# Taking a transition's second root from three sums gathered in the GEMM before it, and merging the residual update into the norm, in a two-block transformer kernel

## What is computed

```
x = x + g_m[:, None, :] * rmsnorm_2(y, norm_g[l, 1])      # y: output of the mixer (short conv, or attention)
h = modulate(rmsnorm_2(x, norm_g[l, 2]), sh_f, sc_f)      # h * (1 + scale) + shift
y = squared_relu_mlp(h, mlp_up_w[l], mlp_down_w[l])
x = x + g_f[:, None, :] * rmsnorm_2(y, norm_g[l, 3])
```

## Time and profile before

| | us |
|---|---|
| median of 3 runs | 1821.46 |
| lowest, highest | 1819.21, 1821.91 |
| the profiled execution | 1821.19 |
| its span | 1818.5 |
| TensorE busy with matmuls | 1780.4 (98%) |
| VectorE busy | 1080.0 (59%) |
| ScalarE busy | 614.1 (34%) |
| GpSimd busy | 80.0 (4%) |

### The profile page before, as it was taken

The page is one execution under the profiler, slowest core; times in us unless marked ns, Lnnn a source line. Parts: engine busy times, 40 slices in busy tenths (PEclk is TensorE's granted clock), DMA queues, the critical chain, the costliest instruction groups (busy, mean ns, idle before and its releaser), DMA issues. The chain is left out here.

```text
span 1818.5 us, 22910 instructions
## 1 busy us (share of the span) xinstructions
PE 1780.4 (98%) x8160; PEld 1426.7 (78%) x8160; DVE 1080.0 (59%) x1556; ACT 614.1 (34%) x951; POOL 80.0 (4%) x132
## 2 busy tenths in 40 slices
PE   9999999999999999999999999999989999999996
PEld 7777677888888878887888888877757788888885
DVE  5566464655655566776656565658766755434354
ACT  4226444322222343223423232425344341323230
POOL 0000000000000000001000000010000100000001
PEclk9999999999999999999999999999999999999998
DMA  6231111444454434552254555422421234333321
GB/s 223 75 108 34 44 41 60 155 161 151 138 169 154 139 93 129 182 186 93 93 188 161 194 165 187 145 70 70 126 72 62 90 107 159 97 93 100 93 81 46
DMA packets 59984, 215.33 MB, mean 118 GB/s; under 512 B 6656, under 2 KB 6656, under 8 KB 59776
## 3 DMA queue, kind: packets, MB, share of 16 engines
q1 hardware_dynamic: 43632, 154.95, 25.5%
q0 software_dynamic: 16128, 58.73, 10.4%
q10 hardware_dynamic: 144, 0.59, 0.1%
HBM read 212.15 MB, written 2.10 MB: 118 GB/s over the span
## 5 line engine op out<-in xcount | busy, mean ns | idle before, releaser
L726 ACT ACTIVATE w_hi<-w_raw 128x1024 fp32r<-128x1024 f32 x285 | 300.6, 1056 | 459.6 <-PE psum L1646 416.8
L1644 PE MATMUL psum<-h_hi,w_hi 128*128 128x512 f32 x1080 | 421.6, 390 | 1.4 <-DVE h_lo L1079 0.9
L1645 PE MATMUL psum<-h_lo,w_hi 128*128 128x512 f32 x1080 | 420.2, 389 | 0.0
L1646 PE MATMUL psum<-h_hi,w_lo 128*128 128x512 f32 x1080 | 420.2, 389 | 0.0
L1048 DVE TENSOR_TENSOR w_lo<-w_raw,w_hi 128x1024 fp32r<-128x1024 f32 x285 | 348.3, 1222 | 110.9 <-ACT w_hi L726 100.7
L1646 PE MATMUL psum<-hid_hi,w_lo 128*128 128x512 f32 x760 | 295.7, 389 | 0.0
L1644 PE MATMUL psum<-hid_hi,w_hi 128*128 128x512 f32 x760 | 295.6, 389 | 0.0
L1645 PE MATMUL psum<-hid_lo,w_hi 128*128 128x512 f32 x760 | 295.6, 389 | 0.0
L1644 PEld LDWEIGHTS psum<-h_hi,w_hi 128*128 128x128 f32 x1080 | 202.7, 188 | 45.2 <-DVE h_lo L1079 1.3
L1645 PEld LDWEIGHTS psum<-h_lo,w_hi 128*128 128x128 f32 x1080 | 202.8, 188 | 42.2 <-issue 0.5
L1646 PEld LDWEIGHTS psum<-h_hi,w_lo 128*128 128x128 f32 x1080 | 202.7, 188 | 41.9
(11 more groups left out here) (279 smaller groups left out, 1933.6 us busy)
## 6 DMA issues: line engine op xcount, KB each, us to landing
w_raw<-in_wstream SPq DMA_DIRECT2D x285, 512.0 KB, 3.6
ada_raw<-in_ada POOLq DMA_DIRECT2D x112, 512.0 KB, 3.8
x<-in_xT SPq DMA_DIRECT2D x8, 256.0 KB, 6.5
outT<-x SPq DMA_DIRECT2D x8, 256.0 KB, 2.1
con<-in_consts SPq DMA_DIRECT2D x1, 1028.0 KB, 10.5
con<-in_rope ACTq DMA_DIRECT2D x1, 576.0 KB, 3.8
par<-in_params SPq DMA_DIRECT2D x1, 259.0 KB, 2.7
```

What stands on the lines that cost most here:

```text
L726: act.activation(w_hi[:, slot, :], w_raw[:, slot, :], ACT.Copy).then_inc(whi_done, 1)
L1644: pe.matmul(bank, w_hi[:, slot, w], hi[:, ra + k, :], start=k == 0, stop=False)
L1645: pe.matmul(bank, w_hi[:, slot, w], lo[:, ra + k, :], start=False, stop=False)
L1646: mm = pe.matmul(bank, w_lo[:, slot, w], hi[:, ra + k, :], start=False, stop=k == nk - 1)
```

## The change

It touches the first and the third transition; the second stays as it was.

The sum of squares of the new x = x + r * b, where b = y * gain and r is the root of y, is written out as sum(x^2) + 2 r sum(x * b) + r^2 sum(b^2). The three sums do not need r, and are gathered in the stage that makes y (`fore`). For each of its eight blocks c: ScalarE squares x[c], y[c] and y[c] * gain; VectorE copies y[c], makes b_mul = y * gain * x and adds y's square of the block before to ss; GpSimd adds the three new products to x_sum, b_sum and g_sum (19 adds in a stage, the last b and g adds are VectorE's). For blocks 6 and 7 ScalarE also multiplies y by the gain in place. The split of w_lo comes after this work instead of before it, and GpSimd issues its ada loads between the adds.

Behind the stage: TensorE takes the means of the three sums (`means`), ScalarE makes the root of y and a copy of it in SBUF, VectorE combines the means (`resum`), ScalarE takes the second root from that. The update is merged into the norm (`renew`): GpSimd finishes tiles 6 and 7 while the root is made, then tiles 1, 3 and 5; VectorE tiles 0, 2 and 4, between its norm operations. The stages squares and sums of squares of the new x go away. In the first transition four modulation groups instead of five come before take, and the group that is left out moves into the MLP (modulation(3) in place of modulation(2) behind its second group); the numbers of warming matmuls are 2 and 8 behind take.

The diff, cut to this (semaphores, counters and the choice of operands in rstd are left out):

```diff
+    def renew(groups, gain, name, shift, more, warm):
+
+
+
+        about = dict(inst=counts["fore"] // DT - 1, old=gain)
+        modulation(1)
+        total(1)
+        add("means", **about)
+        modulation(groups - 1)
+        rstd(EPS2, wide=True, fore=about["inst"] + 1)
+        add("resum", **about)
+        take()
+        gains(name)
+        modulation(more, warm, bank=3)
+        rstd(EPS2, resummed=about["inst"] + 1)
+        r0 = counts["rhs"]
+        add("renew", dict(val=DT, hi=DT, rhs=DT, step=3, xup=3, xpool=5, held=3), dst="h", src="x", src_at=0, nch=DT,
+            dst_at=0, gain=name, shift=shift, splits={}, **about)
+        return r0
...
-    close(5, "r_m0", ("g_f0",), 2, (3, 7))
-    h = norm("h", gain="g_f0", shift=24)
+    gemm("acc", 8, "hid", hid, dst="y", first=True, sq=True, fore="r_m0", rows=8)
+    h = renew(4, "r_m0", "g_f0", 24, 2, 2)
...
-    mlp(h, (0, 12, 12, 8), (16, 16, 16, 0), 2, 1)
+    mlp(h, (0, 12, 12, 8), (16, 16, 16, 0), 3, 1)
...
-    close(3, "r_m1", ("g_f1",), 0, (11, 15))
-    h = norm("h", gain="g_f1", shift=88)
+    h = renew(3, "r_m1", "g_f1", 88, 0, 8)
...
+        y_sq, g_sq, x_sq, b_mul = ([scratch[:, 2 * i + j, :] for j in range(2)] for i in range(4))
+        b_sum, g_sum, x_sum = scratch[:, 8, :], scratch[:, 9, :], rstd[:, :]
+        mean_b, mean_g, mean_x, new_root = (psum[:, i, :] for i in (0, 1, 2, PT_BANK))
+        root_copy, resum = scratch[:, 4, :], scratch[:, 0, :]
+        OWN, ADDED, WHOLE = (0, 2, 4), (1, 3, 5), (6, 7)
...
+                if s.get("fore") and s["kind"] == "gemm":
+                    inst = s["at"]["fore"] // DT
+                    for c in range(DT):
+                        if c >= 1:
+                            pool.wait_ge(fore_x, DT * inst + c + 1)
+                            pool.wait_ge(sum_x, 7 * inst + c - 1)
+                            pool.tensor_tensor(x_sum, x_sq[0] if c == 1 else x_sum, x_sq[c % 2], ALU.add).then_inc(sum_x, 1)
+                        if 1 <= c < DT - 1:
+                            pool.wait_ge(fore_b, DT * inst + c + 1)
+                            pool.wait_ge(sum_b, 6 * inst + c - 1)
+                            pool.tensor_tensor(b_sum, b_mul[0] if c == 1 else b_sum, b_mul[c % 2], ALU.add).then_inc(sum_b, 1)
+                            pool.wait_ge(fore_g, DT * inst + c + 1)
+                            pool.wait_ge(sum_g, 6 * inst + c - 1)
+                            pool.tensor_tensor(g_sum, g_sq[0] if c == 1 else g_sum, g_sq[c % 2], ALU.add).then_inc(sum_g, 1)
+                        upto = min((s["at"]["ada"] + (c + 1) * s["rows"] // DT) // 2 + 2, 4 * ADA_GROUPS)
+                        for v in range(done, upto):
+                            pool.wait_ge(ada_used, 2 * v - 2)
+                            load(v, v % 2)
+                        done = max(done, upto)
+                if s["kind"] == "resum":
+                    pool.wait_ge(root_done, s["inst"] + 1)
+                    for i, c in enumerate(WHOLE):
+                        n = len(WHOLE) * s["inst"] + i + 1
+                        pool.wait_ge(gained_done, n)
+                        pool.tensor_tensor(y[:, c, :], y[:, c, :], root_copy, ALU.mult).then_inc(gained_mul, 1)
+                        pool.wait_ge(gained_mul, n)
+                        pool.tensor_tensor(x[:, c, :], x[:, c, :], y[:, c, :], ALU.add).then_inc(x_pool, 1)
...
+                if s["kind"] == "renew":
+                    for i, c in enumerate(ADDED):
+                        pool.wait_ge(held_done, s["at"]["held"] + i + 1)
+                        pool.tensor_tensor(x[:, c, :], x[:, c, :], y[:, c, :], ALU.add).then_inc(x_pool, 1)
...
+                    if s.get("fore"):
+                        c, inst = t.b, at_["fore"] // DT
+                        if c >= 2:
+                            act.wait_ge(sum_x, 7 * inst + max(c - 2, 1))
+                        act.activation(x_sq[c % 2], x[:, c, :], ACT.Square).then_inc(fore_x, 1)
+                        act.wait_ge(bank_free, BANKS + t.o + 1)
+                        if c >= 2:
+                            act.wait_ge(ss_done, at_["ss"] + c)
+                        act.activation(y_sq[c % 2], y[:, c, :], ACT.Square).then_inc(sqv_done, 1)
+                        act.wait_ge(gains_done, at_["gains"])
+                        if c >= 2:
+                            act.wait_ge(sum_g, 6 * inst + max(c - 2, 1))
+                        act.activation(g_sq[c % 2], y[:, c, :], ACT.Square, scale=gain_of(s["fore"], c)).then_inc(fore_g, 1)
+                        if c in WHOLE:
+                            act.wait_ge(fore_b, DT * inst + c + 1)
+                            act.activation(y[:, c, :], y[:, c, :], ACT.Copy, scale=gain_of(s["fore"], c))\
+                               .then_inc(gained_done, 1)
...
+                    act.activation(new_root if s.get("fore") else wide_root if s.get("wide") else rstd[:, :], log, ACT.Exp,
+                                   scale=-0.5).then_inc(rstd_done, 1)
+                    if s.get("fore"):
+                        act.activation(root_copy, log, ACT.Exp, scale=-0.5).then_inc(root_done, 1)
...
+                    elif evac == "acc" and s.get("fore"):
+                        c, inst = t.b, at_["fore"] // DT
+                        if c >= 1:
+                            dve.wait_ge(sqv_done, at_["sqv"] + c)
+                            dve.wait_ge(ss_done, at_["ss"] + c)
+                            dve.tensor_tensor(ss[:, :], ss[:, :], y_sq[(c - 1) % 2], ALU.add).then_inc(ss_done, 1)
+                        dve.wait_ge(out_done, t.o + 1)
+                        dve.tensor_copy(y[:, c, :], bank).then_inc(bank_free, 1)
+                        dve.wait_ge(bank_free, BANKS + t.o + 1)
+                        if c >= 2:
+                            dve.wait_ge(sum_b, 6 * inst + max(c - 2, 1))
+                        dve.scalar_tensor_tensor(out=b_mul[c % 2], in0=y[:, c, :], scalar=gain_of(s["fore"], c),
+                                                 in1=x[:, c, :], op0=ALU.mult, op1=ALU.mult).then_inc(fore_b, 1)
+                        if c == DT - 1:
+                            dve.wait_ge(sum_b, 6 * (inst + 1))
+                            dve.wait_ge(fore_b, DT * (inst + 1))
+                            dve.tensor_tensor(b_sum, b_sum, b_mul[c % 2], ALU.add).then_inc(sums_done, 1)
+                            dve.wait_ge(sum_g, 6 * (inst + 1))
+                            dve.wait_ge(fore_g, DT * (inst + 1))
+                            dve.tensor_tensor(g_sum, g_sum, g_sq[c % 2], ALU.add).then_inc(sums_done, 1)
+                        split_lo(t.n + AHEAD, (t.n0 + AHEAD) % SPLIT)
...
+            def new_step(s, c):
+
+                out = y[:, c, :] if c in ADDED else psum[:, (PT_BANK + 1, AUX_BANK)[c // 2 % 2], :]
+                dve.scalar_tensor_tensor(out=out, in0=y[:, c, :], scalar=gain_of(s["old"], c), in1=new_root,
+                                         op0=ALU.mult, op1=ALU.mult).then_inc(held_done if c in ADDED else step_done, 1)
+
+            def new_plus(s, c):
+
+                dve.wait_ge(step_done, s["at"]["step"] + OWN.index(c) + 1)
+                dve.tensor_tensor(x[:, c, :], x[:, c, :], psum[:, (PT_BANK + 1, AUX_BANK)[c // 2 % 2], :], ALU.add)\
+                   .then_inc(x_done, 1)
+
+            def resummed(s):
+
+                inst, n = s["inst"], 4 * s["inst"]
+                dve.wait_ge(means_done, 3 * inst + 2)
+                dve.wait_ge(root_done, inst + 1)
+                dve.tensor_tensor(resum, mean_g, root_copy, ALU.mult).then_inc(resum_step, 1)
+                dve.wait_ge(resum_step, n + 1)
+                dve.scalar_tensor_tensor(out=resum, in0=mean_b, scalar=2.0, in1=resum, op0=ALU.mult, op1=ALU.add)\
+                   .then_inc(resum_step, 1)
+                dve.wait_ge(resum_step, n + 2)
+                dve.tensor_tensor(resum, resum, new_root, ALU.mult).then_inc(resum_step, 1)
+                dve.wait_ge(resum_step, n + 3)
+                dve.wait_ge(means_done, 3 * inst + 3)
+                dve.tensor_tensor(resum, resum, mean_x, ALU.add).then_inc(resum_step, 1)
+                dve.wait_ge(resum_step, n + 4)
+                dve.tensor_scalar(resum, resum, 0.0, None, ALU.max).then_inc(resum_done, 1)
+                new_step(s, 0)
+                new_plus(s, 0)
+
+            def renew(s):
+                value, low = norm_steps(s)
+
+                def val(c):
+                    wait_renewed(dve, s, c)
+                    value(c)
+
+                val(0)
+                new_step(s, 1)
+                low(0)
+                new_step(s, 2)
+                val(1)
+                new_plus(s, 2)
+                low(1)
+                new_step(s, 3)
+                val(2)
+                new_step(s, 4)
+                low(2)
+                new_step(s, 5)
+                val(3)
+                new_plus(s, 4)
+                low(3)
```

(35 more changed lines are left out.)

61 lines of the change are left out of this document (38 added, 23 removed).

## The result

The changed kernel takes 1835.05 us (median, 1834.41 to 1836.28), against 1821.54 before (the runs shown before and one more): a ratio of 1.0079, interval 1.0067 to 1.0092. So it is 0.8% slower, where a change too small to tell was forecast: 1819.7, and 1816 to 1823 as the forecast case's own range. The wide range, 1812 to 1845, holds it, since it was drawn to take in the rivals. The profiled span grew by 14.8, from 1818.5 to 1833.3.

A forecast was written before the change was run, and what follows sets the result against it. TensorE, busy 98% of the span, was taken as the bound, so only its waits in two transitions could give time. Terms -1.1 - 1.6 + 0.9 = -1.8 gave 1819.7 us; range 1816 to 1823, with rivals 1812 to 1845.

The forecast's parts named there:

- forecast case: Whole kernel: small gains in the first and third transition, adds free; 1819.7 us, own range 1816 to 1823; chance 40%.
- If all three run undisturbed: nothing: Gathering stages: extra ScalarE passes and GpSimd's 19 adds fit beside TensorE's 5.44 us blocks, at no cost.
- rival 1: Gathering stages and merged norm: VectorE and GpSimd hold each other up; 1843 us (25%), or 1825 if partly (15%).
- its two forms: Whole-instruction blocking, sums falling back 1.76 us per block, 1843 us; or partial blocking, costing 3 to 8 us, 1825.
- Its threshold at 5.44: Gathering stages: blocking decides once a whole-instruction lock makes a block's sum pass 5.44 us; 7.2 us was priced.
- To the first norm value: Behind the stage, from the last copy's start: first norm value at 11.3 us instead of 16.40, 5.1 earlier.
- the five steps: Behind the stage: VectorE's five dependent steps of the new sum take 3.5 us with hand-overs, ending at 8.7.
- The merged norm: First norm value to fourth block: 22.1 us (first transition), 21.6 (third), giving most back; net gains 1.1 and 1.6.
- The moved group: One modulation group moves from the first transition into the MLP, where TensorE works without gaps: +0.9 us.
- Rival 2: Merged norm: VectorE's 23 operations fit under TensorE's 2.05 us per k, each transition keeps 5.1; 1812 us, 13%.
- Rival 3: Wait for take: TensorE idles and its clock falls, perhaps in the third transition; 0 to 2 us, 1820.5, 7%.
- the blocking rivals: VectorE and GpSimd hold each other up: whole-instruction blocking 1843 us, chance 25%; partial blocking 1825 us, chance 15%.

The follow-up runs named there:

- the run without rows: Changed kernel with VectorE's eight modulation rows moved from the first gathering stage into the two convolution stages ahead of it, third stage unchanged: 1832.0 us, ratio 1.0062.
- the kernel before with adds: Kernel before the change plus 19 GpSimd adds on idle tiles in each of the two stages, with nothing waiting for them: 1844.0 us, ratio 1.0128.

## Why the prediction was wrong

- **The step that failed** is "If all three run undisturbed: nothing", the price of GpSimd's 19 adds. They cost 4.9 and 8.4 us of late copies, 12.9 us of the whole time (1835.05 against 1822.15 without them). They stretched VectorE's row by 1.03, ss by up to 1.08 and b_mul by 0.3 to 0.5. By durations VectorE's 4.1 us became 6.5 to 6.7; start to start, 3.8 became 6.3, of a block of 5.44. The forecast case was named over rival 1 because it "alone rests on rows", though no row showed a GpSimd add beside a two-input operation. An operation pair that the trace has never shown side by side is no row for "nothing".
- **Rival 1 was the right mechanism**, in size between its two forms: 0.86 a block instead of 1.76 or nothing, copies 4.9 and 8.4 late instead of 9. It looked for the bound in GpSimd's chain; in the changed kernel it was VectorE's queue, which drains the banks, as the run without rows shows. GpSimd's chain comes next, at 5.64 to 5.78 a block. Its threshold at 5.44 was right, and so was its remark that the third transition has no slack. The rule of the Trainium skill, "SBUF — State Buffer", section "Who interferes with whom", by which the prediction priced 1843, agrees with the runs in who meets whom: operations with two SBUF inputs against GpSimd's reads, and not those with one of the two in PSUM (0.68 and 0.74 beside adds). Its hold for the whole instruction is a little strong: a row beside an add paid 1.03 of the add's 1.27, an add beside w_lo 0.94 of 1.22; what becomes of the rest no run shows. The time came out 15.4 over the forecast's 1819.7, where full exclusion was priced at 24.
- **To the first norm value** I gave 11.3 from the copy. The run without adds took 12.38, the changed kernel 12.8. VectorE reached the sum at 5.50 there (5.3 forecast), the five steps took 4.2 instead of 3.5. The reason is the clamp, taken as 0.48, which ran beside GpSimd's work on y and x and took 1.34 (0.61 and 1.10 in the changed kernel). The clamp has one SBUF input and still paid, so the prediction's short form of the rule, that one SBUF input does not contend, left out a part. The same section of the Trainium skill excepts a mode that uses both ports, and lists tensor_scalar, which the clamp is, among the operations that can enter it. No run here shows in which mode the clamp ran.
- **The merged norm** took 23.7 and 22.9 where 22.1 and 21.6 stood: val(4) started 12.1 behind val(0) instead of 10.8, since h_lo(0) took 1.70 beside the first add and two more h_lo 0.9. That the merged norm gives back most of the gain was right in kind and too small in size: 4.0 and 3.5 of 5.1 stood there, 5.6 and 4.8 of 4.0 and 4.1 were given back, all of it and more. So this second term is wrong apart from the adds: with free sums the forecast gains of 1.1 and 1.6 were losses of 1.6 and 0.7.
- **The moved group**: 0.9 forecast, 1.02 measured; put back, 0.9 returned (334.67 to 333.77).
- **Rival 2**, no give-back, is out: the merged norm took 23.7 where 18.1 would have kept the gain. **Rival 3** came true in mechanism: the clock fell in the wait for take (0.50 in the 860 stretch), and also in a wait for ss that it had not foreseen (0.50 from 846 to 852). It is worth at most 0.2 us, at the low end of its 0 to 2.
- That 1835 lies within 1812 to 1845 is no merit of the forecast case, which was given 40% and 1816 to 1823; it is the blocking rivals, given 40% together, that put the upper end there.

## What to carry to other kernels

Before giving an idle GpSimd elementwise work, list what VectorE does in that stretch with two SBUF inputs, add about one microsecond per meeting at this tile size to VectorE's time per block, and compare with TensorE's block. Then do the same for GpSimd's own chain with its waits. Below the block the adds were all but free, above it every block paid. Count the stretch, not the busy share, which was 61% for a VectorE that was the bound. Where the two must meet, give VectorE's operations a PSUM operand and make GpSimd pause between its operations, and do both. The first alone was worse than nothing (1840.7 against 1835.1). The second alone was not run in the changed kernel; in the kernel before with adds, where GpSimd waits for each add too, every add met a VectorE operation and the time was 1844.0.

## What the runs showed that I had not expected

- A series of GpSimd adds that start without a wait between them kept a fresh VectorE operation out for up to four of them (w_lo 5.31 to 6.04 us instead of 1.22); a wait for its own completion after each add ended that (at most 2.66). In the changed kernel the two took strict turns. That the pause is what lets VectorE in is shown by that edit; why turns are taken in one case and not in the other, beyond that GpSimd's add had itself been kept waiting there, is not.
- An in-place tensor_scalar of 128x512 with one SBUF input took 1.34 us beside GpSimd's operations, where the tensor_scalar of the earlier trace rows takes 0.48.
- Eight modulation rows moved into the short query stages cost 5 us there, though the convolution stages took eight at no cost that shows: the first transition began at 840.99 to 842.59 in the three runs that have them there, and at 841.34 in the changed kernel.
